# Hybrid decoder layer with a routed mixture of experts: a rank-based router, and the rows of the last two experts returned to token order by TensorE

## What is computed

```python
x2 = rms_norm(h, norm2)
g_logits = x2 @ w_rg + b_rg                  # 4 groups, top 1
e_logits = x2 @ w_re + b_re                  # 4 experts in the group, top 2
top_w = softmax(two best e_logits) * softmax(g_logits)[best group]
for e in range(16):                          # a token meets two of them
    out += gates[:, e] * ((silu(x2 @ w_g[e]) * (x2 @ w_u[e])) @ w_d[e])
y = rms_norm(h + out, norm_f)
```

## Time and profile before

| What | Value |
|---|---|
| median of 3 runs | 998.38 us (993.59 to 999.98) |
| the profiled execution | 993.6 us, its span 991.8 us |
| mean granted clock of PE | 0.953 |
| busy: PE / DVE / ACT / POOL | 893.8 / 657.2 / 492.3 / 84.3 us |
| DMA over the whole span | 174.02 MB, mean 175 GB/s |

### The profile page before, as it was taken

The page is one execution under the profiler, slowest core; times in us unless marked ns, Lnnn a source line. Parts: engine busy times, 40 slices in busy tenths (PEclk is TensorE's granted clock), DMA queues, the critical chain, the costliest instruction groups (busy, mean ns, idle before and its releaser), DMA issues.

```text
span 991.8 us, 14556 instructions
## 1 busy us (share of the span) xinstructions
PE 893.8 (90%) x5884; PEld 510.5 (51%) x5884; DVE 657.2 (66%) x864; ACT 492.3 (50%) x684; POOL 84.3 (8%) x90
## 2 busy tenths in 40 slices
PE   5999999999999998999999989617999999999960
PEld 4434784857666555444444479513444444444420
DVE  3677769533886776543443255455899999988916
ACT  6434373324445444333233325524888887777812
POOL 7000000003000000000000000020111112321100
PEclk9989999999999999999999989757999999999995
DMA  8712414437310115933423360185999999999606
GB/s 207 168 29 63 109 35 115 129 86 149 86 32 17 38 38 179 305 104 102 117 85 91 85 210 5 64 315 179 327 392 387 384 378 360 370 370 362 270 25 251
DMA packets 147247, 174.02 MB, mean 175 GB/s; under 512 B 14391, under 2 KB 99695, under 8 KB 147174
## 3 DMA queue, kind: packets, MB, share of 16 engines
q1 hardware_dynamic: 139760, 158.56, 47.8%
q0 software_dynamic: 7136, 13.89, 5.0%
q10 hardware_dynamic: 278, 0.56, 0.2%
HBM read 168.30 MB, written 13.07 MB: 183 GB/s over the span
## 4 chain that ended last, share of the span: by engine, by line
PE 79%; DMA 10%; DVE 7%; ACT 3%; issue 1%; POOLq 0%; SPq 0%; DVEq 0%; ACTq 0%
PE bank L916 22%; PE bank L917 21%; PE bank L918 21%; DMA arena<-in_moe_wu 7%; PE bank L1128 3%; PE bank L1147 3%; PE bank L1022 1%; PE bank L1137 1%; PE bank L1285 1%; DVE arena L1646 1%; DMA arena<-x_rows,token_of 1%; ACT arena L801 1%; PE bank L1219 1%; DMA arena<-in_x 1%; PE bank L1007 1%
## 5 line engine op out<-in xcount | busy, mean ns | idle before, releaser
L916 PE MATMUL bank<-arena 128*128 128x512 f16 (+1 forms) x1568 | 464.9, 317 | 13.1 <-DVE arena L1393 4.6
L917 PE MATMUL bank<-arena 128*128 128x512 f16 (+1 forms) x1568 | 464.1, 316 | 0.0
L918 PE MATMUL bank<-arena 128*128 128x512 f16 (+1 forms) x1568 | 463.8, 316 | 0.0
L1646 DVE SCALAR_TENSOR_TENSOR arena<-arena 128x2048 f16<-128x2048 f32 x96 | 217.1, 2288 | 46.7 <-ACT arena L801 46.7
L916 PEld LDWEIGHTS bank<-arena 128*128 128x128 f16 x1568 | 155.0, 99 | 141.2 <-issue 33.5
L918 PEld LDWEIGHTS bank<-arena 128*128 128x128 f16 x1568 | 154.7, 99 | 111.3 <-issue 3.0
L917 PEld LDWEIGHTS bank<-arena 128*128 128x128 f16 x1568 | 154.7, 99 | 100.0 <-issue 2.8
L801 ACT ACTIVATE arena<-arena 128x2048 f16<-128x2048 f32 x96 | 182.1, 1909 | 44.1 <-PE bank L918 14.6
L568 ACT ACTIVATE arena<-arena 128x1024 f16<-128x1024 f32 (+1 forms) x92 | 92.5, 1007 | 102.0 <-PE bank L918 73.5
L1393 DVE SCALAR_TENSOR_TENSOR arena<-arena 128x1024 f16<-128x1024 f32 (+1 forms) x91 | 103.5, 1163 | 11.7 <-ACT arena L568 10.1
L622 ACT ACTIVATE arena<-bank 128x512 f32<-128x512 f32 x35 | 20.8, 595 | 90.7 <-PE bank L918 90.6
(11 more groups left out here) (257 smaller groups left out, 735.1 us busy)
## 6 DMA issues: line engine op xcount, KB each, us to landing
arena<-in_moe_wg SPq DMA_DIRECT2D x32, 1024.0 KB, 13.7
arena<-in_moe_wu SPq DMA_DIRECT2D x32, 1024.0 KB, 15.0
arena<-in_moe_wd SPq DMA_DIRECT2D x32, 1024.0 KB, 15.1
arena<-in_w_gate SPq DMA_DIRECT2D x32, 512.0 KB, 4.2
arena<-in_w_in SPq DMA_DIRECT2D x31, 512.0 KB, 3.9
arena<-in_w_branch SPq DMA_DIRECT2D x32, 192.0 KB, 3.6
arena<-in_w_out SPq DMA_DIRECT2D x8, 512.0 KB, 5.1
arena<-y_rows SPq DMA_DIRECT2D x4, 1024.0 KB, 8.6
```

The costliest lines, as they stand in the source:

```text
L916: pe.matmul(outb, lhs[0], rhs[0], start=first, stop=False, skip_group_check=True)
L917: pe.matmul(outb, lhs[0], rhs[1], start=False, stop=False, skip_group_check=True)
L918: return pe.matmul(outb, lhs[1], rhs[0], start=False, stop=last_, skip_group_check=True)
L1646: tell("split_done", stt(w_lo[c % NW], stage[c % NS], WSCALE, w_hi[c % NW], ALU.mult, ALU.subtract))
```

## The change

1. **Router.** The logits of all four tiles go to one bank (`ps[6]`). DVE compares each logit with the three others of its group in 320-element instructions, sums the defeats into a place, and has `sel16` after ten instructions; the two choices, their logits and the weights are worked out later. `dense_known` is signalled as soon as the counts are there.
2. **Near and far.** A small one-hot table for experts 0 and 1 only gives their `token_of`; the full table and all other numbers are made after the low half of expert 0's rows (`x_lo(0)`), multiplied by PE between steps 1 and 2 (`all_tokens`) and read by DVE at step 2 (`all_slots`). ACT does not wait for `token_full` before splitting chunks 5 and 6; its first tanh waits for `token_full` 2.
3. **SP.** Chunks 8 to 12 are issued before the stores of x2, as soon as each split allows. Four DMAs of 1 MB that write zeros (a row of c_tab, read over and over) to `y_rows` stand before the loads of chunks 40 to 43 of the mixer block.
4. **Order of steps.** The two down steps of expert 13 come before the u steps of expert 14; the transposes of h of experts 13 and 15 move to (g, 14, 1) and (d, 14, 1).
5. **End.** Only experts 0 to 13 are scattered. Their rows are loaded after expert 13's scatter, and DVE adds them at steps 91 to 94. The results of experts 14 and 15, scaled by the token's weight, stay in SBUF as float16 pairs (`y16`); PE multiplies them by transposed one-hot tables (128 slots x 512 tokens, made by DVE at step 32): 32 products, 12 of them before the low halves of expert 15. DVE adds the sums to h, and the norm follows as before. A square root on ACT after the last tanh brings its table in early.

The diff, cut to its core (beat, place, etop, slotw, tok_iota are new small tiles):

```diff
+W16 = 1024.0
+LAST = 2
+NEAR = 2
+ROUTED = NE - LAST
+_at = STEPS.index(("u", ROUTED, 0))
+STEPS[_at:_at + 4] = STEPS[_at + 2:_at + 4] + STEPS[_at:_at + 2]
+H_AT = {}
+for _e in range(NE):
+    if _e == ROUTED - 1:
+        H_AT["g", _e + 1, 1] = _e
+    elif _e == NE - 1:
+        H_AT["d", _e - 1, 1] = _e
+    else:
+        H_AT["u", _e + 1, 0] = _e
...
@@ SP
+                if CEND["cv"] + AHEAD <= c < CEND["cv"] + 2 * AHEAD:
+                    i = c - CEND["cv"] - AHEAD
+                    nothing = bass.AP(d["c_tab"].tensor, d["c_tab"].offset + (BUCKETS + 2) * (T + P), [(0, 2 * P), (1, D)])
+                    sp_.dma_start(y_rows[2 * P * i:2 * P * (i + 1), :], nothing).then_inc(S(f"tokens_in{i}"), 16)
                 mixer_load(c)
...
+            for c in range(NS, NS + FIRST):
+                sp_.wait_ge(S("split_done"), c - NS + 1)
+                stage_load(c)
             for t in range(NT):
                 sp_.wait_ge(S("x2_ready"), t + 1)
                 sp_.dma_start(x2_rows[t * P:(t + 1) * P, :], xs[:, t, :]).then_inc(S("x2_stored"), 16)
-            for c in range(NS, NS + FIRST):
-                sp_.wait_ge(S("split_done"), c - NS + 1)
-                stage_load(c)
...
                 for i in range(2):
-                    sp_.wait_ge(S(f"y_stored{i}"), 16 * (NE // 2))
-                sp_.wait_ge(S("split_done"), len(STEPS))
+                    sp_.wait_ge(S(f"y_stored{i}"), 16 * (ROUTED // 2))
+                sp_.wait_ge(S("split_done"), len(STEPS) - NS + NT)
@@ POOL
-                for n in range(NE + 4):
+                for n in range(NE + 2):
...
-                        if e < 2:
+                        if e < NEAR:
                             pool.wait_ge(S("xg_clear"), 1)
+                            pool.wait_ge(S("token_read"), 1)
                         else:
+                            pool.wait_ge(S("token_read"), 2)
                             pool.wait_ge(S("xgT_full"), 2 * (e - 1))
@@ ACT
-            act.wait_ge(S("token_full"), 1)
             for c in range(FIRST, NW):
                 split(c)
...
                     if kind == "g" and hf:
                         act.wait_ge(S("chunk_used"), steps_to("g", e))
+                        if e == 0:
+                            act.wait_ge(S("token_full"), 2)
...
+                        if e == NE - 1:
+                            link(act.activation(stat[:, 2, 0:1], ones[:, 0:1], ACT.Sqrt))
...
+                            else:
+                                act.wait_ge(S("token_read"), 2)
+                                act.activation(y16[e % 2][0][:, 512 * j:512 * (j + 1)], y_bank(e)[j][:, :], ACT.Copy,
+                                               scale=slotw[:, e - ROUTED:e - ROUTED + 1]).then_inc(S("y_out"), 1)
@@ PE
+                def all_tokens():
+                    pe.wait_ge(S("onehot_ready"), 1 + NT)
+                    for e in range(NE):
+                        for t in range(NT):
+                            last = pe.matmul(ps[4][:, 5 * e:5 * e + 5], onehot[:, t, :].rearrange("p (c e) -> p e c", e=NE)[:, e, :],
+                                             told[:, t, :, e], start=(t == 0), stop=(t == NT - 1))
+                    last.then_inc(S("token_full"), 1)
...
+                    if c == 1:
+                        all_tokens()
...
+                def put_back(t, i):
+                    for j in range(2):
+                        for part in range(2):
+                            last = pe.matmul(sum_bank[t][j][:, :], onehot_T[i][:, t * P:(t + 1) * P],
+                                             y16[(ROUTED + i) % 2][part][:, 512 * j:512 * (j + 1)], ...
+                pe.wait_ge(S("onehot_ready"), 1 + NT + LAST)
+                pe.wait_ge(S("ylo_done"), 2)
+                for t in range(NT - 1):
+                    put_back(t, 0)
+                pe.wait_ge(S("ylo_done"), 4)
+                for t in range(NT):
+                    if t == NT - 1:
+                        put_back(t, 0)
+                    put_back(t, 1).then_inc(S("sum_full"), 1)
@@ DVE
+            link(tt(rlog[:, :, :], ps[6][:, 0:NT * nr]..., stat[:, 3, :]..., ALU.mult))
+            link(tt(rlog[:, :, :], rlog[:, :, :], rbias..., ALU.add))
+            link(tt(tied, other, own, ALU.is_ge))
+            link(tt(ahead, other, own, ALU.is_gt))
+            link(tt(tied, tied, lower..., ALU.mult))
+            link(tt(ahead, ahead, tied, ALU.max))
+            link(dve.tensor_reduce(place[:, 0, ...], ahead, axis=AX.X, op=ALU.add))
+            link(ts(place[:, 1, :, :, :], place[:, 0, :, :, :], 0.5, None, ALU.is_lt))
+            link(ts(place[:, 2, :, :, :], place[:, 0, :, :, :], 1.5, None, ALU.is_lt))
+            sig("sel_ready", tt(sel16..., place[:, 2, :, 1:, :], group, ALU.mult))
...
+            sig("onehot_ready", tt(onehot_near, slots.rearrange("p (c e) -> p c e", e=NE)[:, :, 0:NEAR]..., rank..., ALU.is_equal))
...
+            sig("token_read", dve.tensor_copy(token_of[:, 0:NEAR], slotv[:, 1, 0:NEAR]))
+            for c in range(FIRST, NW):
+                split(c)
             dve.wait_ge(S("rt_exp"), 2)
...
+                ROWS_AT = dict(zip((steps_to("u", NE - 1) - 1, steps_to("d", NE - 2) - 2, steps_to("d", NE - 2) - 1,
+                                    len(STEPS) - 2), range(NT)))
+                def add_rows(t):
+                    dve.wait_ge(S(f"tokens_in{t}"), 48)
+                    for j in range(2):
+                        link(stt(hres[:, t, :], yg[t][:, j, :], wsel[:, j, t:t + 1], hres[:, t, :], ALU.mult, ALU.add))
+                def y_lo(e):
+                    for j in range(2):
+                        dve.wait_ge(S("y_out"), 2 * e + j + 1)
+                        tell("ylo_done", stt(y16[e % 2][1]..., y_bank(e)[j][:, :], slotw..., y16[e % 2][0]..., ALU.mult, ALU.subtract))
...
                 x_lo(0)
+                dve.wait_ge(S("x2_stored"), 16 * NT)
+                for t in range(NT):
+                    tell("onehot_ready", tt(*onehot_views(t), ALU.is_equal))
                 for c, (kind, e, hf) in enumerate(STEPS):
+                    if c == 2:
+                        all_slots()
...
+                    if c == 4 * NE // 2:
+                        dve.wait_ge(S("gain2_landed"), 48)
+                        for i in range(LAST):
+                            tell("onehot_ready", ts(onehot_T[i], tok_iota, slotv[:, 1, ROUTED + i:ROUTED + i + 1], None, ALU.is_equal))
+                    if c in ROWS_AT:
+                        add_rows(ROWS_AT[c])
+                    if kind == "d" and hf and e >= ROUTED:
+                        y_lo(e)
...
+                def add_last(t):
+                    dve.wait_ge(S("sum_full"), t + 1)
+                    for j in range(2):
+                        h_ = hres[:, t, 512 * j:512 * (j + 1)]
+                        ins = tt(h_, sum_bank[t][j][:, :], h_, ALU.add)
```

215 lines of the change are left out of this document (117 added, 98 removed).

## The result

The changed kernel takes 987.5 us as the median of 8 runs (985.58 to 991.2); the kernel before, on the same chip, 997.4 (993.59 to 1001.89, 8 runs). The ratio is 0.991, 95% interval 0.9886 to 0.9934. The profiled execution took 987.6 us with a span of 985.8, where before it was 991.8: 6.0 us shorter, and 24.5 had been summed.

The account below looks back on a forecast made before the run. PE was taken to bound the expert stage first, the DMAs later, with DVE close behind. Gains of 9.9 (start), 1.3 (lead), 1.6 (order) and 11.7 (end) summed to 24.5 us, forecasting 973 us, range 962 to 985.

Parts of the forecast that it names:

- Order: Last experts: 2.4 us gained at expert 15's h, 0.8 (0 to 2) lost at expert 13's, together 1.6 gained.
- the branch 1.0 (0 to 2.2, POOL's whole distance): VectorE's queue before `x_lo(0)`: entering the routed part costs 1.0 us, bounded by POOL's time from `dense_known` to the gather.
- the router doesn't do what it says: Rival at the start: row gather holds up `x_lo(0)`, half the start's gain is lost, 980 us; chance 0.05.
- 24 products at 0.43: 5.1 late: Rival at steps 2 and 3: moved small matmuls let PE's clock fall, products take 0.43 for 0.216, 978 us; chance 0.08.
- at full clock they may take half: 64 small matmuls between steps 1 and 2: 2.1 to 4.1 us, taken 3.1, against 4.13 at clock 0.50.
- The end: 20.8 for 19.8: From last product to end of span: 19.8 us instead of 31.5, so 11.7 gained (9 to 13).
- ACT's chain may show more: Reason given for the bounds of 9 to 13 us on the 11.7 gained after the last product.
- the selection: Router on DVE: selection ready 3.9 us after the logits, with 0.48 us for each 320-element instruction.
- the gather: Start of expert 0: fetching its rows takes 5 us (bounds 3.2 and 8.1), where it took 8.10.
- the middle of the expert stage: Expert stage: one chunk more of lead wins back 1.3 us (0 to 2.7) of the 8.3 lost to late chunks.
- the zero fills: Mixer block: cost nothing, bound 7 us late; rival: slow one-place reads, 15 us each, give 1024 us; chance 0.03.
- The small one-hot table: Router on DVE: 1024 elements take between 0.6 and 1.1 us, taken 1.1 because slot numbers lie 16 apart.

Follow-up runs that it names:

- cover: Changed kernel with h of expert 13 transposed at (g, 14, 0) and expert 15's rows behind expert 13's second down step: 982.55 us, ratio 0.9854.
- fall: Changed kernel with VectorE's routed branch standing first, entered by running on, using a flag of its own: 984.37 us, ratio 0.9886.
- branch: Changed kernel with VectorE's branch right after `token_read`; weights and splits of chunks 5 and 6 moved into both branches: 979.27 us, ratio 0.9836.
- tables: On top of `branch`: the 64 small matmuls before step 0 and the full tables before `x_lo(0)`: 981.11 us, ratio 0.985.
- order: Changed kernel with the old step order and expert 13's h at (u, 14, 0) again; expert 15's h stays early: 984.04 us, ratio 0.9873.
- again: The changed kernel run once more without any edit, for a second profile: 987.87 us, ratio 0.9921.
- fills: Changed kernel with the zero fills moved four chunks later, behind the bias loads: 985.8 us, ratio 0.9894.
- sqrtboth: Changed kernel with the early square root at the end of both ScalarE branches, not only the routed one: 985.83 us, ratio 0.9896.

## Why the prediction was wrong

The range ended at 985, the result is 987.5: the direction and most of the mechanisms were right, their sum was over twice the truth. The 18.5 us between the 24.5 summed and the 6.0 of the profiled executions lie in five places.

- **The end of the expert stage: +5.4 instead of -1.6, 7.0 of the 18.5.** The step that failed is "Order". It looked at the wait that the new order removes, and at h of expert 13, for which it put 0.8 (0 to 2) and the trace shows 2.96. Behind those transposes there are 12 products, 2.6 us, and VectorE had four splits in front of the low half (8.89 us in one piece, 917.90 to 926.79). And it didn't see at all that the moved down steps were also the cover for `x_lo(15)`: in the old order two down steps stand between the transposes of the next expert's rows and its first product, in the new one nothing does before expert 15. That is 2.65. `cover` takes out just these two, and gets 5.5 back. Behind the first of them the clock was low for eight products, 1.7. A step list shows this without a chip: write down, for each handed-over block, how many products lie between its transposes and its first use, before and after.
- **VectorE's branch: 6.6 for 1.0, 5.4 of the 18.5.** The step that failed is "the branch 1.0 (0 to 2.2, POOL's whole distance)". The bound was taken from another engine's distance, and it was treated as a bound for a thing that no row of VectorE showed. It didn't show in the kernel before because the branch stood in a place where VectorE waited for rows anyway (6.82 idle). `fall`, which removes the jump (and adds one small instruction for its flag), brings the first product 5.4 forward; `branch`, which hides it and moves the splits too, 6.9. The rival "the router doesn't do what it says" had the size (half of the start's gain) but put it on the row gather, which took 5.4 us and wasn't late.
- **The small matmuls and the clock behind them, 2.3.** That was a rival at 0.08, "24 products at 0.43: 5.1 late". It came true in part, with the clock at 0.80 from 676 to 682 and at 0.60 from 690 to 694. The matmuls took 3.91 (taken 3.1, bounds 2.1 to 4.1). The step that failed there is "at full clock they may take half": 64 of them take 4.12 us at a clock of 0.50 (`tables`) and 4.07 at 1.00 (`order`), so the 4.13 of the earlier trace rows should have been carried over whole. Both together cost 2.3 us over the sum in the changed kernel, 2.4 in `again`, and 1.5 less than that in `fills` (57.1 us to expert 2's transposes). Since the earlier trace rows had shown the low clock with just these instructions, part of its price belonged in the sum.
- **The mixer block, 2.9.** No part of the change. The forecast carried 4.8 us for the median's own spread, and that is where this lies.
- **The end: 20.8 for 19.8.** The first addition comes 3.5 us behind the last product (forecast 3.6). The missing 1.0 is ScalarE's table load at 972.53 (`sqrtboth` gets 1.1 back), which the bound "ACT's chain may show more" held.

What was right, by the same steps: the selection 3.9 us after the logits (3.9), with 0.49 for each 320-element instruction (0.48); the gather 5.4 us (5); the middle of the expert stage 1.3 better (1.3); rows landed in time at all four additions; the zero fills without the 7 us or more that their rival needed. The small one-hot table took 1.07 us for 1024 elements (1.1 taken). Its slot numbers are taken in pairs that lie 16 apart; the full table, with whole rows of 16, takes 1.16 us for 2048 elements, nearly twice the rate. It isn't quite the single rate either: from 0.49 us for 320 elements and 0.69 for 512 I estimate 1.22 for 1024 at the single rate. By the Trainium skill, "VectorE: DVE Perf Modes", section "What auto-detection actually checks", as the prediction read it, step 1 inside the pairs would have sufficed for the double rate; the trace disagrees, and the 1.1 that the prediction took held. One slip of the sum: 998.38 less 24.5 is 973.9, and 973 was forecast.

What stays open: what decides the clock in the mixer block from one execution to the next, behind which of two waits of about 3 us the clock falls, and whether and by how much the chunk loads lengthen the stall behind a jump.

## What to carry to other kernels

A saving at the start of a chain is worth what the next thing on the same engine lets through: before a queue is moved up, list what stands in it that the trace showed only as waiting (a branch, a value read), and give those a price from a measurement or a wide bound. When steps are put in another order, count for every hand-over the products that cover it; the wait that goes is easy to see in the trace, the covers that go are not in it at all. Three small repairs of that kind (where the branch stands, two transposes one step away, the same table at the end of both branches) made the change worth 25 us instead of 10.

## What the runs showed of the hardware that was not expected

- A taken jump over a long branch held VectorE for 3.87 us with nearly idle DMA engines and for 6.3 to 7.5 beside 1 MB loads, and where the jump is taken out (`fall` for the changed kernel) the instruction queue has 3 packets instead of 6 from 640 to 700 us; a branch over a few instructions 1.19 us; entering the branch that stands first 1.04 us.
- The granted clock of TensorE from 225 to 250 us was 0.93 in six profiled executions and 1.00 in eight, with the same instructions there in all but two (the kernel before, and the fills moved): with the second such stretch 2.5 us of a span of 990.
- 64 matmuls of 5 columns took 4.12 us at a granted clock of 0.50 and 4.07 us at 1.00: their time didn't follow the clock.
- The clock fell to half behind TensorE waits of 2.96 us (changed kernel), 2.60 (`cover`), 1.97 (`order`) and 2.65 (`fills`, `fall`), and stayed at 1.00 behind one of 3.31 (`fills`).
- ScalarE loaded a table (1.28 us) for the first instruction behind the join of two branches although the branch taken had left the right one.
